# Moving the turns of probabilities and values inside the k and q units of a first attention

## The chip, the cores and the metric

One NeuronCore of a Trainium2 chip runs the whole program. The metric is the device time of one execution in microseconds. The four compute engines named here are TensorE (PE, with its weight loads shown as PEld), VectorE (DVE), ScalarE (ACT) and GpSimd (POOL); SyncE (SP) issues most of the DMAs. Every engine takes its instructions in the order in which the program wrote them for it, and they wait for one another through semaphores.

## The reference

Two transformer blocks in float32 for 512 tokens of width 1024. The change touches only the first block's differential attention, 8 heads, each with two softmaxes of 64 columns over causal scores; their difference multiplies 128 columns of values:

```python
qb = q.reshape(bsz, nb, Q_BLOCK, N_HEADS, 2, HEAD_DIM).transpose(1, 0, 2, 3, 4, 5)
def one_block(args):
    qblk, bi = args
    s = jnp.einsum('bqhcd,bkhcd->bhcqk', qblk, k).astype(jnp.float32) * scale
    s = jnp.where(mask, s, neg)
    p = jax.nn.softmax(s, axis=-1)
    a = p[:, :, 0] - lam * p[:, :, 1]
    return jnp.einsum('bhqk,bkhe->bqhe', a.astype(v.dtype), v)
# before it: q and k = rope(rmsnorm(q or k of the projection)), 64 columns at a time
# behind it: o = rmsnorm(o, subln_gain) * (1 - lam_init), then the output projection
```

## The kernel before

Work on TensorE comes in **units**: one unit is a 128-column slice of a projection, `named(name, ...)` or `tile` (L543), 8 slices k of the contraction with 3 matmuls of 512 columns each (L559 to L561; high and low halves of weights and activations), 24 matmuls into one of two PSUM banks `pg`. `ahead_of(k)` is called in front of each k. ScalarE splits a unit's weights into high and low halves three units ahead (`ahead`, `hi`, L1079 and L1080), GpSimd issues the accumulating DMA that makes the low half (L523), and SP loads raw weights and swaps halves of k and q for the rope (L495, L496).

The first attention is a loop over h from 1 to 9 with the units k, q and v of head h (gate units where no head is left) and, between them, the attention of head g = h - 1. Each engine has its own copy of the loop, and its order is written out by hand. The names of head g's steps:

- `scores(g, i)` (L733, L735): scores of query block i, two softmaxes, with the causal mask; it needs q after rope (`roped`) and a free bank `ps`. There are two banks `ps`; scores and turns take them in turn, so scores 0 and turn 2 of the head before share one, scores 2 and turn 0 share one, scores 1 and turn 3, scores 3 and turn 1.
- `maximum` (L1839) on VectorE, then `exps1` (L1221) on ScalarE, then `combine` (L1845, L1561, L1558; four instructions, result `pa`, semaphore `combed`) on VectorE.
- `turn(g, i)` (L743): i + 1 transposes of the combined block on TensorE into a bank `ps`; `turned` copies it to `pt`, turns 0 and 2 on ScalarE (L1233), turns 1 and 3 on VectorE (L1856).
- the values' turn (L801): four transposes of `v_raw` into `px`, copied by ScalarE (L1302).
- the product (L811): probabilities and values of head h - 2 into `py`; it waits for the copies of turns 2 and 3. ScalarE squares and copies `py` (L1311, L1312).
- `kq_out` (L1241, L1242): ScalarE's two evacuations of a k or q unit; `kq_rest` (two VectorE operations) makes the rest of its squares, `kq_sums` (L761, L762) sums them, `head_root` (L1252, L1254) takes the root; `rope_step` (four VectorE operations) applies it. The same for the output norm: `o_rest`, `o_sums` (L754, L755), L1248, and the product with the root on VectorE (L1558, `hid`).

The order before, per loop step h. TensorE: unit k; turns 2 and 3 of head h - 2; values' turn; scores 0 and 1; product of head h - 2; unit q; turns 0 and 1; sums of k; sums of the output norm; scores 2 and 3; unit v; sums of q. ScalarE: split; `kq_out` of k; copy of turn 2; copy of values; exponentials 0 and 1; copies of the product; split; `kq_out` of q; copy of turn 0; roots of k and of the output norm; exponentials 2 and 3; split; v; root of q. VectorE: copy of turn 3; rest of k; maxima 0 and 1; combines 0 and 1; rest of the output; copy of turn 1; rest of q; output norm; maxima 2 and 3; rope of k; combines 2 and 3; rope of q.

Of the kernel before, what the change touches and what calls it, by code (L numbers as in the profile page):

```python
# [7 lines left out]
P = 128  # L8
# [3 lines left out]
HEADS = 8  # L12
# [182 lines left out]
def build(nc, weights, x_dram, consts, rope, masks, params, ssm_b, ssm_c, lru_w, out):  # L195
    with ExitStack() as ctx:
# [209 lines left out]
        def evacuated(eng, name):  # L406

            eng.wait_ge(pg_free[TILE[name] % 2], TILE[name] // 2 + 1)
# [133 lines left out]
        def _(pe):  # L542
# [21 lines left out]
            def named(name, xh, xl, **kw):  # L564
                tile(UNIT[name], TILE[name], xh, xl, **kw)
# [33 lines left out]
            def x_use(name):  # L599
                if XUSE[name] > 0:  # L600
                    pe.wait_ge(px_free, XUSE[name])
# [126 lines left out]
            def scores(h, i):  # L728
                bank, w = s_use(("s", h, i)), P * (i + 1)
                pe.wait_ge(roped, 2 * h + 2)  # L730
                for c in range(2):
                    r = slice(64 * c, 64 * c + 64)
                    pe.matmul(bank[:, c, 0:w], qq[r, h % 2, P * i:P * i + P], kk[r, h % 2, 0:w], start=True, stop=False)  # L733
                for c in range(2):
                    last = pe.matmul(bank[:, c, P * i:w], ident_b, msk[:, M_TRI:M_TRI + P], start=False, stop=True)  # L735
                last.then_inc(ps_full, 1)

            def turn(h, i):

                bank = s_use(("t", h, i))  # L740
                pe.wait_ge(combed, 4 * h + i + 1)
                for j in range(i + 1):
                    last = pe.transpose(bank[:, 0, P * j:P * j + P], pa[:, i % 2, P * j:P * j + P], ident)  # L743
                last.then_inc(ps_full, 1)
# [37 lines left out]
                    pe.wait_ge(blocks_made, 1)  # L782
                    kq_sums(0, "k", 0)
            kq_sums(0, "q", 1)
            for h in range(1, HEADS + 2):
                g = h - 1
                attends = g < HEADS
                if h < HEADS:
                    named(("k", h), XH, XL)
                elif h == HEADS:  # L790
                    named(("gate", 4), XH, XL)
                else:
                    named(("gate", 7), XH, XL)
                if h >= 2:
                    turn(h - 2, 2)
                    turn(h - 2, 3)
                if attends:
                    x_use(("vt", g))
                    evacuated(pe, ("v", g))
                    for j in range(QB):  # L800
                        last = pe.transpose(px[:, P * j:P * j + P], v_raw[:, P * j:P * j + P], ident)  # L801
                    last.then_inc(px_full, 1)
                    scores(g, 0)
                    scores(g, 1)
                if h >= 2:
                    y_use(("pv", h - 2))
                    px_read(pe, ("vt", h - 2))
                    ps_read(pe, ("t", h - 2, 2))
                    ps_read(pe, ("t", h - 2, 3))
                    for j in range(QB):  # L810
                        last = pe.matmul(py[:, P * j:T], vv[:, h % 2, j, :], pt[:, j, P * j:T],  # L811
                                         start=j == 0, stop=j == QB - 1)
                    last.then_inc(py_full, 1)
                if h < HEADS:
                    named(("q", h), XH, XL)
                elif h == HEADS:
                    named(("gate", 5), XH, XL)
                if attends:
                    turn(g, 0)
                    turn(g, 1)  # L820
                if h < HEADS:
                    kq_sums(h, "k", 0)
                if 2 <= h <= HEADS:
                    o_sums(h - 2)
                if attends:
                    scores(g, 2)
                    scores(g, 3)
                if h < HEADS:
                    named(("v", h), XH, XL)
                    kq_sums(h, "q", 1)  # L830
                if h == HEADS:
                    named(("gate", 6), XH, XL)
# [229 lines left out]
        def _(act):  # L1062
# [198 lines left out]
                free(act.activation(hid[:, m], a, ACT.Sigmoid, bias=par("b_glu", m)), ("glu", m))  # L1261

            def late_gate(g):
                ahead(("gate", g))
                free(act.activation(gates[:, g], done(("gate", g)), ACT.Copy), ("gate", g))

            ahead(("k", 0))
# [22 lines left out]
            for h in range(1, HEADS + 2):  # L1290
                g = h - 1
                attends = g < HEADS
                if h < HEADS:
                    ahead(("k", h))
                    kq_out(h, "k", 0, "kg")
                else:
                    late_gate(4 if h == HEADS else 7)
                if h >= 2:
                    turned(h - 2, 2)
                if attends:  # L1300
                    px_ready(("vt", g))
                    act.activation(vv[:, g % 2], px[:].rearrange("p (j d) -> p j d", d=P), ACT.Copy).then_inc(px_free, 1)  # L1302
                    exps1(g, 0)
                    exps1(g, 1)
                if h == HEADS + 1:
                    act.wait_ge(maxed, EXPS[("s", HEADS - 1, QB - 1)] + 1)
                    for o in (5, 6):
                        o_high(o)
                if h >= 2:
                    py_ready(("pv", h - 2))  # L1310
                    put(act.activation(sq_hi[2] if h <= HEADS else nrm[:, 0], py[:], ACT.Square), o_sq)  # L1311
                    act.activation(hid[:, h - 2], py[:], ACT.Copy).then_inc(py_free, 1)  # L1312
                if h < HEADS:
                    ahead(("q", h))
                    kq_out(h, "q", 1, "qg")
                if h == HEADS:
                    late_gate(5)
                if attends:
                    turned(g, 0)
                if h == HEADS:  # L1320
                    for o in range(2):
                        o_high(o)
                if h < HEADS:
                    head_root(("ssq_k", h), 0, C_EPS, 1.0 / 64, rs_k)
                if h >= 2:
                    if h >= 3:
                        act.wait_ge(o_done, h - 2)
                    head_root(("ssq_o", h - 2), 2, C_EPS, 1.0 / P, rs_o)
                if attends:
                    exps1(g, 2)  # L1330
                    exps1(g, 3)
                if h < HEADS:
                    ahead(("v", h))
                    free(act.activation(v_raw[:], done(("v", h)), ACT.Copy), ("v", h))

                    head_root(("ssq_q", h), 1, C_EPS64, 1.0, rs_q)
                if h == HEADS:
                    for o in range(2, 5):
                        o_high(o)
                    late_gate(6)  # L1340

            o_high(HEADS - 1)
# [190 lines left out]
        def _(dve):  # L1533
# [366 lines left out]
            for h in range(1, HEADS + 2):  # L1900
                g = h - 1
                attends = g < HEADS
                if h >= 2:
                    turned(h - 2, 3)
                if h < HEADS:
                    kq_rest(h, "k", 0)
                if attends:
                    maximum(("s", g, 0), P, 0, soft)
                    maximum(("s", g, 1), 2 * P, 1, soft)
                    combine(g, 0)  # L1910
                    combine(g, 1)
                if 2 <= h <= HEADS:
                    o_rest(h - 2)
                if attends:
                    turned(g, 1)
                if h < HEADS:
                    kq_rest(h, "q", 1)
                if h == HEADS:
                    for o in range(2):
                        o_low(o)  # L1920
                if h == HEADS + 1:
                    for o in (5, 6):
                        o_low(o)
                if h >= 2:
                    py_read(dve, ("pv", h - 2))
                    dve.wait_ge(rs_o, h - 1)
                    put(stt(hid[:, h - 2], hid[:, h - 2], lam_t[:, 6:7], kq_rs[:, 2]), o_done)
                if attends:
                    maximum(("s", g, 2), 3 * P, 2, soft)
                    maximum(("s", g, 3), 4 * P, 3, soft)  # L1930
                if h < HEADS:
                    rope_step(h, "k", 0, rs_k, kk)
                if attends:
                    combine(g, 2)
                    combine(g, 3)
                if h < HEADS:
                    rope_step(h, "q", 1, rs_q, qq)
                if h == HEADS:
                    for o in range(2, 5):
                        o_low(o)  # L1940
# [361 lines left out]
```

## Time and profile before

| | |
|---|---|
| median of 3 runs | 1423.48 us (1423.08 to 1425.09) |
| the profiled execution | 1422.14 us, span 1420.3 us |
| TensorE busy | 1398.5 us, 98% of the span |
| ScalarE busy | 832.2 us, 59% |
| VectorE busy | 698.4 us, 49% |
| GpSimd busy | 202.0 us, 14% |
| granted TensorE clock | 0.999 |

A busy time is the sum of an engine's instructions over the span. Matmuls are pipelined: the duration of one (0.39 us) is longer than the distance to the next (0.23 us), so costs on TensorE are read from distances between starts, and idle time in brackets is what lies behind the modelled end of the instruction before.

### The profile page before, as it was taken

The numbers are of one execution on the slowest core, as the hardware profiler recorded it, in microseconds if no ns is written. First come the engines' busy times: TensorE is split into PE (matmuls) and PEld (weight loads), VectorE is DVE, ScalarE is ACT, GpSimd is POOL, SyncE is SP. The second block draws the span as 40 slices with busy tenths as digits, with TensorE's granted clock in tenths as the row PEclk, the third lists the DMA queues.
The fourth block names the chain that finished last, engine by engine and source line by source line (L and its number), as shares of the span: only waits on it lengthen the run. The fifth ranks groups of instructions, "written<-read, shape, count | busy, mean of one in ns | idle before, by whom it ended". The sixth has DMA issues, their size and how long they took to land.

```text
span 1420.3 us, 18417 instructions
## 1 busy us (share of the span) xinstructions
PE 1398.5 (98%) x6734; PEld 1121.1 (79%) x6734; DVE 698.4 (49%) x1228; ACT 832.2 (59%) x1174; POOL 202.0 (14%) x236
## 2 busy tenths in 40 slices
PE   7999999999999999999999999999999999999998
PEld 5887877777778888888888887777788888888887
DVE  6992477877734455544154165757465301213324
ACT  7536566776755656665365477645756655535442
POOL 1210100100111111111111111010101111111111
PEclk9999999999999999999999999999999999999999
DMA  9996966566579888888878997754667898888873
GB/s 298 221 188 154 233 156 141 132 156 142 115 197 220 193 188 193 187 202 192 214 177 187 214 233 158 160 139 108 145 153 162 193 202 192 190 202 180 206 163 89
DMA packets 82692, 254.76 MB, mean 179 GB/s; under 512 B 16816, under 2 KB 20016, under 8 KB 82608
## 3 DMA queue, kind: packets, MB, share of 16 engines
q0 software_dynamic: 32400, 117.98, 46.2%
q1 hardware_dynamic: 48768, 132.50, 30.9%
q10 hardware_dynamic: 1440, 3.15, 0.6%
q8 instruction: 54, 0.88, 0.3%
q14 instruction: 30, 0.25, 0.0%
HBM read 128.03 MB, written 3.41 MB: 93 GB/s over the span
## 4 chain that ended last, share of the span: by engine, by line
PE 94%; DVE 3%; ACT 2%; issue 0%; DMA 0%; DVEq 0%; ACTq 0%
PE pg L559 27%; PE pg L561 27%; PE pg L560 27%; PE ps L733 2%; PE py L811 1%; PE ps L947 1%; PE ps L957 1%; ACT pairs_r L1241 1%; PE py L967 1%; DVE acc L1558 1%; PE ps L735 0%; ACT kq_raw L1242 0%; PE ps L949 0%; DVE acc L1555 0%; PE px L632 0%
## 5 line engine op out<-in xcount | busy, mean ns | idle before, releaser
L559 PE MATMUL pg<-x_hi,w_hi 128*128 128x512 f32 x1088 | 429.0, 394 | 0.0
L561 PE MATMUL pg<-x_hi,w_lo 128*128 128x512 f32 x1088 | 424.0, 390 | 0.0
L560 PE MATMUL pg<-x_lo,w_hi 128*128 128x512 f32 x1088 | 423.5, 389 | 0.0
L523 POOL DMA_DIRECT2D w_lo<-w_raw x225 | 194.0, 862 | 1186.3 <-ACT w_lo L1080 1134.9
L1079 ACT ACTIVATE w_hi<-w_raw 128x1024 fp32r<-128x1024 f32 x222 | 233.4, 1051 | 100.9 <-PE pg L561 99.8
L559 PEld LDWEIGHTS pg<-x_hi,w_hi 128*128 128x128 f32 x1088 | 204.3, 188 | 43.5 <-issue 1.6
L561 PEld LDWEIGHTS pg<-x_hi,w_lo 128*128 128x128 f32 x1088 | 204.2, 188 | 43.0
L560 PEld LDWEIGHTS pg<-x_lo,w_hi 128*128 128x128 f32 x1088 | 204.4, 188 | 42.5 <-issue 1.0
L1080 ACT ACTIVATE w_lo<-w_raw 128x1024 fp32r<-128x1024 f32 x222 | 232.3, 1046 | 0.0
L559 PE MATMUL pg<-act_hi,w_hi 128*128 128x512 f32 x424 | 165.0, 389 | 0.0
L561 PE MATMUL pg<-act_hi,w_lo 128*128 128x512 f32 x424 | 165.0, 389 | 0.0
L560 PE MATMUL pg<-act_lo,w_hi 128*128 128x512 f32 x424 | 165.0, 389 | 0.0
L559 PEld LDWEIGHTS pg<-act_hi,w_hi 128*128 128x128 f32 x424 | 79.6, 188 | 16.8 <-DMA w_lo<-w_raw 0.2
L561 PEld LDWEIGHTS pg<-act_hi,w_lo 128*128 128x128 f32 x424 | 79.6, 188 | 16.6
L560 PEld LDWEIGHTS pg<-act_lo,w_hi 128*128 128x128 f32 x424 | 79.6, 188 | 16.3
L1555 DVE TENSOR_TENSOR cu<-pg,rstd 128x512 f32<-128x512 f32 x44 | 30.4, 691 | 114.6 <-PE pg L561 112.9
L1555 DVE TENSOR_TENSOR pairs<-rel 128x512 f32<-128x512 f32 x30 | 20.8, 692 | 129.5 <-ACT rel L1500 129.5
L1555 DVE TENSOR_TENSOR hid<-hid,pg 128x512 f32<-128x512 f32 x32 | 22.0, 687 | 102.8 <-PE pg L561 98.8
L1558 DVE SCALAR_TENSOR_TENSOR cnv<-cu,prm,cnv 128x511 f32<-128x511 f32 x88 | 66.0, 750 | 3.1
L1555 DVE TENSOR_TENSOR acc<-acc,pg 128x512 f32<-128x512 f32 (+1 forms) x24 | 16.2, 676 | 92.1 <-PE pg L561 91.3
L1221 ACT ACTIVATE pr<-ps,soft 128x128 f32<-128x128 f32 (+3 forms) x64 | 33.2, 523 | 27.1 <-DVE soft L1839 26.4
L1839 DVE TENSOR_REDUCE soft<-ps 128x2 f32<-128x256 f32 (+3 forms) x48 | 39.6, 824 | 6.7 <-PE ps L949 4.1
(384 smaller groups left out, 1743.9 us busy)
## 6 DMA issues: line engine op xcount, KB each, us to landing
w_raw<-weights SPq DMA_DIRECT2D x226, 512.0 KB, 4.8
w_lo<-w_raw POOLq DMA_DIRECT2D x225, 512.0 KB, 5.7
kq_rot<-kq_raw SPq DMA_DIRECT2D x64, 64.0 KB, 3.3
hid<-x SPq DMA_DIRECT2D x4, 512.0 KB, 5.4
hid<-x ACTq DMA_DIRECT2D x8, 256.0 KB, 5.3
out<-hid SPq DMA_DIRECT2D x16, 128.0 KB, 1.8
u_dram<-hid SPq DMA_DIRECT2D x4, 256.0 KB, 5.4
pairs<-u_dram SPq DMA_DIRECT2D x8, 128.0 KB, 6.8
```

The source lines that it names most:

```text
L523: pool.dma_start(w_lo[:, s], w_raw[:, s], accum_op=ALU.add).then_inc(lo_in[s], 16)
L559: pe.matmul(bank[:], wh, xh(k), start=n == 0, stop=False)
L560: pe.matmul(bank[:], wh, xl(k), start=False, stop=False)
L561: last = pe.matmul(bank[:], wl, xh(k), start=False, stop=n == len(ks) - 1)
L733: pe.matmul(bank[:, c, 0:w], qq[r, h % 2, P * i:P * i + P], kk[r, h % 2, 0:w], start=True, stop=False)
L811: last = pe.matmul(py[:, P * j:T], vv[:, h % 2, j, :], pt[:, j, P * j:T], start=j == 0, stop=j == QB - 1)
L1079: act.activation(w_hi[:, s], w_raw[:, s], ACT.Copy)
L1080: put(act.activation(w_lo[:, s], w_raw[:, s], ACT.Copy, scale=-1.0), hi_done)
L1221: ins = act.activation(dst[:, c, 0:w], bank[:, c, 0:w], ACT.Exp, bias=negmax[:, i % 2, c:c + 1], **kw)
L1555: return dve.tensor_tensor(out_, a, b, op)
L1558: return dve.scalar_tensor_tensor(out_, a, s, b, op0, op1)
L1839: put(dve.tensor_reduce(s[:, i % 2, 0:2], bank[:, :, 0:w], AX.X, ALU.max, negate=True), maxed)
```

## The change

Three orders are changed, one per engine; no instruction of arithmetic is added or dropped. TensorE: turns 2 and 3 of head h - 2 and the values' turn are called in front of k = 6 of unit k, turns 0 and 1 of head g in front of k = 7 of unit q, and the product comes ahead of scores 0 and 1. ScalarE: the copies of turn 2 and of the values come ahead of k's evacuations, the copy of turn 0 ahead of q's. VectorE: maxima 0 and 1 come ahead of the rest of k's squares. `late_gate` no longer calls `ahead`; its callers do.

```diff
+            def values_of(h):
                 if h >= 2:
                     y_use(("pv", h - 2))
...
+            for h in range(1, HEADS + 2):
+                g = h - 1
+                attends = g < HEADS
+
+                def last_turns(k):
+                    if k != 6:
+                        return
+                    if h >= 2:
+                        turn(h - 2, 2)
+                        turn(h - 2, 3)
+                    if attends:
+                        x_use(("vt", g))
+                        evacuated(pe, ("v", g))
+                        for j in range(QB):
+                            last = pe.transpose(px[:, P * j:P * j + P], v_raw[:, P * j:P * j + P], ident)
+                        last.then_inc(px_full, 1)
+
+                def first_turns(k):
+                    if k == 7 and attends:
+                        turn(g, 0)
+                        turn(g, 1)
+
+                named(("k", h) if h < HEADS else ("gate", 4 if h == HEADS else 7), XH, XL, ahead_of=last_turns)
+                values_of(h)
                 if attends:
-                    turn(g, 0)
-                    turn(g, 1)
+                    scores(g, 0)
+                    scores(g, 1)
+                if h <= HEADS:
+                    named(("q", h) if h < HEADS else ("gate", 5), XH, XL, ahead_of=first_turns)
                 if h < HEADS:
                     kq_sums(h, "k", 0)
...
             for h in range(1, HEADS + 2):
                 g = h - 1
                 attends = g < HEADS
-                if h < HEADS:
-                    ahead(("k", h))
-                    kq_out(h, "k", 0, "kg")
-                else:
-                    late_gate(4 if h == HEADS else 7)
+                ahead(("k", h) if h < HEADS else ("gate", 4 if h == HEADS else 7))
                 if h >= 2:
                     turned(h - 2, 2)
                 if attends:
                     px_ready(("vt", g))
                     act.activation(vv[:, g % 2], px[:].rearrange("p (j d) -> p j d", d=P), ACT.Copy).then_inc(px_free, 1)
+                if h < HEADS:
+                    kq_out(h, "k", 0, "kg")
+                else:
+                    late_gate(4 if h == HEADS else 7)
+                if attends:
                     exps1(g, 0)
                     exps1(g, 1)
...
+                if h <= HEADS:
+                    ahead(("q", h) if h < HEADS else ("gate", 5))
+                if attends:
+                    turned(g, 0)
                 if h < HEADS:
-                    ahead(("q", h))
                     kq_out(h, "q", 1, "qg")
                 if h == HEADS:
                     late_gate(5)
-                if attends:
-                    turned(g, 0)
-                if h == HEADS:
                     for o in range(2):
                         o_high(o)
...
                 if h >= 2:
                     turned(h - 2, 3)
+                if attends:
+                    maximum(("s", g, 0), P, 0, soft)
+                    maximum(("s", g, 1), 2 * P, 1, soft)
                 if h < HEADS:
                     kq_rest(h, "k", 0)
                 if attends:
-                    maximum(("s", g, 0), P, 0, soft)
-                    maximum(("s", g, 1), 2 * P, 1, soft)
                     combine(g, 0)
                     combine(g, 1)
```

## Rows read from the trace of the kernel before

**Rows 1.** The page: its span, and the chain that ended last by engine

```profile
span 1420.3 us, 18417 instructions
...
PE 94%; DVE 3%; ACT 2%; issue 0%; DMA 0%; DVEq 0%; ACTq 0%
```

**Rows 2.** Stretches: busy us and count per engine, clock, DMA share, GB/s; head 4

```profile
258.00:284.00 26.00, 25.55 (x126) 18.97 (x125) 20.17 (x37) 18.52 (x38) 2.57 (x4) 1.00 0.62 142
```

**Rows 3.** Timeline, TensorE, head 4: start, duration, engine, line, operation, idle before

```profile
258.41 0.93 PE L743 MATMUL ps<-cst,pa 128*128 128x128 f32 x7
...
259.17 0.60 PE L801 MATMUL px<-cst,v_raw 128*128 128x128 f32 x4
...
260.13 0.49 PE L733 MATMUL ps<-kk,qq 64*128 64x128 f32 x4 [0.36 <-ACT pt L1233]
...
263.66 0.48 PE L559 MATMUL pg<-x_hi,w_hi 128*128 128x512 f32 x1
...
263.97 0.40 PE L560 MATMUL pg<-x_lo,w_hi 128*128 128x512 f32 x1
...
269.24 0.49 PE L743 MATMUL ps<-cst,pa 128*128 128x128 f32 x3
...
269.49 0.47 PE L761 MATMUL px<-pairs_r,blocks 128*128 128x512 f32 x1
...
270.75 0.92 PE L733 MATMUL ps<-kk,qq 64*128 64x384 f32 x4
...
272.96 0.48 PE L559 MATMUL pg<-x_hi,w_hi 128*128 128x512 f32 x1
...
284.42 0.92 PE L743 MATMUL ps<-cst,pa 128*128 128x128 f32 x7
```

**Rows 4.** Timeline, TensorE, head 8: values' turn and scores 0

```profile
363.20 0.60 PE L801 MATMUL px<-cst,v_raw 128*128 128x128 f32 x4
363.73 0.49 PE L733 MATMUL ps<-kk,qq 64*128 64x128 f32 x4
```

**Rows 5.** Timeline, TensorE, head 1: scores 2

```profile
192.71 0.92 PE L733 MATMUL ps<-kk,qq 64*128 64x384 f32 x4 [0.55 <-ACT pt L1233]
```

**Rows 6.** Timeline, VectorE, from the output norm in head 4 to head 5

```profile
273.30 0.75 DVE L1558 SCALAR_TENSOR_TENSOR hid<-hid,lam_t,kq_rs 128x512 f32<-128x512 f32 x1 [1.25 <-ACT kq_rs L1254]
274.08 2.22 DVE L1839 TENSOR_REDUCE soft<-ps 128x2 f32<-128x768 f32 x2
...
281.77 0.75 DVE L1558 SCALAR_TENSOR_TENSOR pa<-pr,soft 128x512 f32<-128x512 f32 x1
282.56 0.75 DVE L1558 SCALAR_TENSOR_TENSOR rope_a<-kq_raw,prm,rtab 128x512 f32<-128x512 f32 x1
...
285.45 0.69 DVE L1856 COPY pt<-ps 128x512 f32<-128x512 f32 x1
286.18 0.69 DVE L1555 TENSOR_TENSOR pairs<-kq_raw 128x512 f32<-128x512 f32 x1
```

**Rows 7.** Timeline, ScalarE, head 4, behind the q unit

```profile
269.44 0.60 ACT L1241 ACTIVATE pairs_r<-pg 128x512 fp32r<-128x512 f32 x1 [2.52 <-PE pg L561]
...
270.41 0.28 ACT L1233 ACTIVATE pt<-ps 128x128 f32<-128x128 f32 x1
...
272.54 0.63 ACT L1254 ACTIVATE kq_rs<-kq_rs 128x512 f32<-128x512 f32 x1
```

**Rows 8.** Timeline, VectorE and TensorE, head 9: last copy and product

```profile
388.11 0.69 DVE L1856 COPY pt<-ps 128x512 f32<-128x512 f32 x1 [3.29 <-PE ps L743]
...
388.95 2.39 PE L811 MATMUL py<-pt,vv 128*128 128x512 f32 x8 [0.94 <-DVE pt L1856]
```

**Rows 9.** Timeline, VectorE, head 8: maximum 1 and the end of combine 1

```profile
365.39 0.69 DVE L1839 TENSOR_REDUCE soft<-ps 128x2 f32<-128x512 f32 x1 [0.43 <-PE ps L735]
...
368.13 0.48 DVE L1558 SCALAR_TENSOR_TENSOR pa<-pr,soft 128x256 f32<-128x256 f32 x1
```

**Rows 10.** Timeline, VectorE, head 1: the last operation of q's rope

```profile
204.88 0.69 DVE L1555 TENSOR_TENSOR qq<-rope_a,kq_rs 128x512 f32<-128x512 f32 x1
```

More of the change, by code:

```diff
@@ L784, in _ @@
             kq_sums(0, "q", 1)
-            for h in range(1, HEADS + 2):
-                g = h - 1
-                attends = g < HEADS
-                if h < HEADS:
-                    named(("k", h), XH, XL)
-                elif h == HEADS:
-                    named(("gate", 4), XH, XL)
-                else:
[L793 to L796, printed above, removed]
-                if attends:
[L798 to L804, printed above, removed]
+            def values_of(h):
                 if h >= 2:
@@ L813, in _ @@
                     last.then_inc(py_full, 1)
[L814 to L817, printed above, removed]
+            for h in range(1, HEADS + 2):
[19 more added lines that the diff above has]
+                values_of(h)
                 if attends:
-                    turn(g, 0)
-                    turn(g, 1)
+                    scores(g, 0)
+                    scores(g, 1)
+                if h <= HEADS:
+                    named(("q", h) if h < HEADS else ("gate", 5), XH, XL, ahead_of=first_turns)
                 if h < HEADS:
@@ L1263, in late_gate @@
             def late_gate(g):
-                ahead(("gate", g))
                 free(act.activation(gates[:, g], done(("gate", g)), ACT.Copy), ("gate", g))
@@ L1292, in _ @@
                 attends = g < HEADS
-                if h < HEADS:
-                    ahead(("k", h))
-                    kq_out(h, "k", 0, "kg")
-                else:
-                    late_gate(4 if h == HEADS else 7)
+                ahead(("k", h) if h < HEADS else ("gate", 4 if h == HEADS else 7))
                 if h >= 2:
@@ L1317, in _ @@
                     late_gate(5)
-                if attends:
-                    turned(g, 0)
-                if h == HEADS:
                     for o in range(2):
@@ L1339, in _ @@
                         o_high(o)
+                    ahead(("gate", 6))
                     late_gate(6)
```

## The prediction

> **What bounds the kernel now.** I read the page's chain that ended last first: 94% of it lies on TensorE, in a span of 1420.3 us [rows 1]. Only what shortens TensorE's stream can shorten the kernel. The change touches one stretch, the first attention (178 to 391 us), so the second view is the table of stretches: one head takes 26.00 us, TensorE is busy in 25.55 of it at full granted clock (1.00), VectorE in 20.17, ScalarE in 18.52 [rows 2]. Six stretches of 26.00 between 206 and 362 look like it. TensorE has almost no idle time there, so the whole prize is a few tenths per head, and a chain through VectorE that is busy 78% of the time can take it back.
>
> The third view is TensorE's timeline in one head [rows 3]. Behind the k unit stand seven turns of probabilities (258.41 to 259.17, 0.76), four turns of values, the scores 0 and 1, and the product of probabilities and values. The scores begin at 260.13, 0.96 after the values' turns. In head 8 the same step is 0.53 [rows 4]. The difference, **0.43 us, is a wait** for ScalarE's copy L1233, which comes behind the two evacuations of k on ScalarE. Behind the q unit the turns take 0.25 (269.24 to 269.49), and from there to the scores 2 it is 1.26 us, where four sum matmuls stand. The first of them costs 0.31, as 263.66 to 263.97 shows for a matmul behind such a block, and the others some 0.235: 1.01. The rest is **a wait of 0.24** for the same line. In head 1, with two sums, it is 0.71: the row shows 0.55 of idle behind the modelled end of the last sum, and a modelled end lies 0.16 behind the end of issue (0.39 against 0.23) [rows 5].
>
> **What each part of the change does on TensorE.** No instruction of arithmetic is added or removed; all of them move. I count starts, so a block's cost is the distance between its first row and the next block's.
>
> - The turns of probabilities and values go in front of k = 6 of the k unit, with 6 matmuls behind them. They cost what they do now, but without the pause between value turns and scores: 0.76 + 0.36 = 1.12 instead of 0.76 + 0.53. Going back to unit matmuls costs once more what it costs at 263.66, where the second matmul comes 0.31 after the first instead of 0.227: 0.08, and some hundredths behind it, 0.11 in all. TensorE therefore pays 1.23 instead of 1.72 (with the wait of 0.43). Bounds of the restart: 0 (no restart), and 0.13, by which a fresh unit (263.66 to 269.24, 5.58) is longer than a k unit of 24 x 0.227 = 5.45.
> - The turns 0 and 1 go in front of k = 7 of the q unit: 0.25 + 0.10 of restart. In exchange the sums behind the unit run at 0.235 each (0.94) instead of 1.01 + 0.24 of wait, since ScalarE copies the turned block before it evacuates q.
> - The product of probabilities and values is put ahead of the scores: same length, 260.13 to 263.66 = 3.53 for both together.
>
> If nothing else waited, a head would be 1.23 + 3.53 + 5.58 + 0.35 + 0.94 + 2.21 (scores 2 and 3, 270.75 to 272.96) + 11.46 (v unit, q sums, k unit, 272.96 to 284.42) = **25.30 against 26.01 now** (258.41 to 284.42): 0.71 less.
>
> **What is late next.** The product needs the block turned last, and its copy is VectorE's (L1856). Today it has time: the scores stand between. In the changed order only six matmuls do. On VectorE this copy comes behind the whole rope step of q, and the rows from 273.30 to 285.45 stand without a gap: output norm, maxima 2 and 3, rope of k, combine 2 and 3 (done at 282.52), rope of q, copy until 286.14 [rows 6]. That is 12.84 us, and the change moves nothing in it. It starts when ScalarE has finished the root for the output norm. Take Q as the end of issue of the q unit (269.24). ScalarE starts on it 0.20 later and ends the last root (272.54 + 0.63) at Q + 3.93 [rows 7]; without the 128-column copy between them, some 0.15 (270.41 to 270.56, where the next operation begins), at Q + 3.78; VectorE starts 0.13 behind: Q + 3.91. The copy is then done at Q + 16.75. From a copy's end to the product it was 0.15 in head 9 (388.80 to 388.95) [rows 8], so the product can start at **Q + 16.90**. TensorE gets there at Q + 0.94 + 2.21 + 11.46 + 1.23 = **Q + 15.84**. So it waits 1.06 us, and a head takes 25.30 + 1.06 = **26.36, 0.35 more than now**. The two waits removed (0.67) come back as one larger wait, because the loop (root, norm, maxima, two ropes, copy, product, scores, q unit) is closed: what TensorE saves elsewhere in the head only makes it arrive earlier at this wait. Queued behind the waiting product are the scores 0 and 1 and so the next maxima; VectorE's idle time moves there, since the rest of k's squares is now behind the maxima.
>
> A second place is close. Turn 1, in front of k = 7, needs combine 1. Counted from the start of scores 0: maximum 1 is done 2.39 later (363.73 to 366.12, which is 365.39 + 0.69 and a gap of 0.04) [rows 4, 9]; then the rest of k's squares, two operations of 0.69 with gaps, 1.42 [rows 6]; then two combines, 366.12 to 368.61 [rows 9]: 6.30, and 0.15 of latency. TensorE asks at 1.39 + 4.90 (21 matmuls, 5.58 less three at 0.227) + 0.11 = 6.40. That is a wait of 0.05 per head. Its bounds are 0 and 0.3.
>
> The other queues: ScalarE's weight split for the unit three ahead moves at most 1.7 us later in the q unit, and it is needed some 26 us later; POOL and SP follow it with the same reserve. k's evacuation waits for TensorE's unit end and is not behind anything by then. I cost these at nothing; the cover is those 26 us.
>
> **The sum by heads**, against the profiled execution.
> Head 1: 0.71 of wait gone, 0.07 and 0.08 at the two joints saved, 0.10 of restart paid, -0.76. Head 2: VectorE's chain starts without the output norm and its wait, rope of q ends at 205.57, some 14.1 us behind the q unit of head 1 [rows 10]; with the copy and the latency that is 15.0, and TensorE asks at 15.4: -0.71. Heads 3 to 7: +0.35 to +0.40 each, +1.9. Head 8 has no wait of 0.43 today (its k unit is a gate unit with one evacuation) but gets the 1.06: +1.06 - 0.06 there, -0.13 behind the q unit, +0.87. Head 9: today the product waits 1.1 for the same copy (0.94 of it idle in the row, 0.16 up to the end of issue) [rows 8], and VectorE, idle for 3.29 before, can only begin it when the turn is there; in the changed kernel the turns come 1.47 ahead of the product (six matmuls and the restart), and begin to end of the copy with its latencies is 1.1: -1.07 with the restart. Total: -0.76 - 0.71 + 1.9 + 0.87 - 1.07 = **+0.2 us**; with the bounds above (restarts of 0 in eight heads, 0.3 for turn 1 in eight heads), -1.5 to +2.5. I take +0.5, as small restarts and latencies have been counted low more easily than high. The profiled execution took 1422.14 us (1420.3 of span), and the median of the runs is 1423.48, 1.34 more; the forecast is made for the median: 1423.48 + 0.5 = **1424.0 us**. About 0.2%, 2.85 us, is what a measurement of this kernel can tell from no change.
>
> **Rivals.**
> *The waits simply go.* If VectorE's copy is not behind the rope of q in time, or the chain starts earlier than Q + 3.91, the product finds its block ready. Then head 1 gives 0.76, heads 2 to 7 give 0.71 each, head 8 gives 0.19, head 9 1.07: 6.3 less, 1417.2 us; with half of the wait left, 1420. For it: TensorE holds 94% of the chain and its idle rows name only ScalarE's copy. Against it: the rows without a gap on VectorE. The Trainium skill (Perfetto Trace Analysis, "Identifying the Most-Contended Engine") says to optimize the engine with the highest occupancy first, and its next section to follow the gaps on it; by that rule the gaps named here are the gain, and the 78% on VectorE would not decide. The rows of the chain speak against that here. Chance 0.13.
>
> *Slower through the first combine.* The rest of k's squares now stands between maximum 1 and combine 0, and turn 1 in front of k = 7 has a reserve of nothing. From the first tenth by which the exponentials or the combine come later than counted, TensorE stands still inside the q unit, one for one. If it is 0.4 per head, as much as one wait for L1233 costs today, eight heads pay 3.2: 1427.2 us. Its place is the first turn with line L743 inside the q unit, its releaser VectorE. For it: nothing is left in reserve. Against it: in the changed order ScalarE has nothing else between the maxima and the exponentials, and VectorE gives it the 1.42 us of k's squares as a lead. Chance 0.14.
>
> **How the numbers follow.** Forecast case 0.73, its own range 1422.3 to 1426.3; full or half gain 0.13; slower 0.14. The range 1420.3 to 1426.9 leaves out about one in ten on each side. Faster by over 0.2% 0.13, within 0.73, slower 0.14.
>
> **What would show it.** Right: heads 3 to 8 with a period near 26.4, no idle time in front of the scores, and about 1 us in front of the product (L811's code) with VectorE's copy as releaser, right behind the rope's last operation; head 9 without a wait. Wrong: a period of 25.3 (the chain on VectorE does not hold), or idle time in front of the turns inside the q unit (the second rival), or a changed time in stretches behind 391 us, for which I have no cause.

## The result and the profile after

| | before | changed |
|---|---|---|
| median | 1423.26 us (20 runs, 1422.42 to 1425.09) | 1425.69 us (20 runs, 1424.6 to 1426.84) |
| ratio to before, 95% interval | | 1.0016 [1.0009, 1.0022] |
| span of the profiled execution | 1420.3 us | 1422.4 us |
| start of the output projection behind the attention | 391.10 us | 393.13 us |
| one head, heads 3 to 7 | 26.00 us | 26.63 us |
| from the output projection's start to the end of the span | 1029.2 us | 1029.3 us |

The changed kernel is 2.4 us, 0.16%, slower. That is inside the 0.2% that the prediction called no change, but the interval lies wholly above 1: the slowdown is small and real. In the traces 2.0 of the 2.1 us lie in the first attention; behind it they run alike.

The page of the changed kernel, its span and its chain by engine:

```profile
span 1422.4 us, 18413 instructions
...
PE 87%; DVE 9%; ACT 2%; issue 1%; DMA 0%; SPq 0%; DVEq 0%; ACTq 0%
```

TensorE's share of the chain fell from 94% [rows 1] to 87% and VectorE's rose from 3% to 9%: a chain through VectorE has become part of what ends last. The table of waits for TensorE between 175 and 400 us (engine, line, whom it waited for: total, times, longest) names it:

```profile
PE py L793 <- DVE pt L1862: 4.1, 6, 0.7
PE pg L559 <- DVE pairs_r L1561: 0.4, 1, 0.4
```

Six waits of the product (L793 here, L811 before) for VectorE's copy of the block turned last (L1862, before L1856), one in each of the heads 3 to 8. The wait for ScalarE's copy in front of the scores is gone. In TensorE's timeline, from head 4 to head 5, against [rows 3]:

```profile
256.93 0.93 PE L743 MATMUL ps<-cst,pa 128*128 128x128 f32 x7
...
270.11 0.39 PE L761 MATMUL px<-pairs_r,blocks 128*128 128x512 f32 x1
...
270.62 0.47 PE L754 MATMUL py<-pairs_r,blocks 128*128 128x512 f32 x1
270.93 0.40 PE L755 MATMUL py<-sq_lo,blocks 128*128 128x512 f32 x1
271.25 0.92 PE L733 MATMUL ps<-kk,qq 64*128 64x384 f32 x4
...
283.56 0.93 PE L743 MATMUL ps<-cst,pa 128*128 128x128 f32 x7
...
284.68 0.48 PE L559 MATMUL pg<-x_hi,w_hi 128*128 128x512 f32 x1
...
287.00 2.39 PE L793 MATMUL py<-pt,vv 128*128 128x512 f32 x8 [0.68 <-DVE pt L1862]
289.33 0.49 PE L733 MATMUL ps<-kk,qq 64*128 64x128 f32 x4
...
290.70 0.47 PE L559 MATMUL pg<-x_hi,w_hi 128*128 128x512 f32 x1
...
295.57 0.63 PE L743 MATMUL ps<-cst,pa 128*128 128x128 f32 x3
295.96 0.48 PE L559 MATMUL pg<-x_hi,w_hi 128*128 128x512 f32 x1
```

Seven turns come at 256.93 and again at 283.56: 26.63. The six matmuls behind the values' turns (from 284.68, 1.47 us) would be through at 286.15; the product starts at 287.00, a wait of 0.85 (0.68 behind the modelled end). VectorE in the same stretch, against [rows 6]:

```profile
269.78 0.69 DVE L1561 TENSOR_TENSOR sq_lo<-pairs,pairs_r 128x512 fp32r<-128x512 f32 x1
...
274.00 0.75 DVE L1564 SCALAR_TENSOR_TENSOR hid<-hid,lam_t,kq_rs 128x512 f32<-128x512 f32 x1 [1.09 <-ACT kq_rs L1259]
274.79 2.22 DVE L1845 TENSOR_REDUCE soft<-ps 128x2 f32<-128x768 f32 x2
...
283.26 0.75 DVE L1564 SCALAR_TENSOR_TENSOR rope_a<-kq_raw,prm,rtab 128x512 f32<-128x512 f32 x1
...
286.16 0.69 DVE L1862 COPY pt<-ps 128x512 f32<-128x512 f32 x1
290.14 0.42 DVE L1845 TENSOR_REDUCE soft<-ps 128x2 f32<-128x256 f32 x1 [3.29 <-PE ps L735]
```

The copy ends at 286.85 and the product follows 0.15 later. With Q, the end of issue of the q unit, at 270.11, where the sums begin, the norm starts at Q + 3.89, the copy is done at Q + 16.74 and the product starts at Q + 16.89. VectorE then stands idle for 3.29 us, because the scores are queued behind the waiting product.

Where the 2.0 us between the traces come from, by the starts of the k units:

| | before | changed | difference | predicted |
|---|---|---|---|---|
| head 1 | 22.67 | 22.23 | -0.44 | -0.76 |
| head 2 | 26.01 | 25.72 | -0.29 | -0.71 |
| heads 3 to 7 | 130.03 | 133.13 | +3.10 | +1.9 |
| head 8 | 24.63 | 25.45 | +0.82 | +0.87 |
| head 9, to the output projection | 9.48 | 8.30 | -1.18 | -1.07 |

### The profile page after: what moved, and what is told of

Its sections match the earlier page's. It is cut to its first block, busy times and chain, and to the rows that moved or that the text cites. A ratio compares the mean times of both kernels' runs of the same rounds, so it can differ in the third digit from the quotient of the medians.

```text
span 1422.4 us, 18413 instructions
## 1 busy us (share of the span) xinstructions
PE 1399.6 (98%) x6730; PEld 1119.5 (79%) x6734; DVE 698.2 (49%) x1228; ACT 834.3 (59%) x1174; POOL 202.0 (14%) x236
## 4 chain that ended last, share of the span: by engine, by line
PE 87%; DVE 9%; ACT 2%; issue 1%; DMA 0%; SPq 0%; DVEq 0%; ACTq 0%
PE pg L559 26%; PE pg L561 26%; PE pg L560 26%; PE py L793 1%; DVE soft L1845 1%; PE ps L733 1%; PE ps L952 1%; PE ps L962 1%; DVE rope_a L1564 1%; DVE rope_a L1561 1%; DVE pa L1564 1%; DVE kq_rot L1564 1%; PE py L972 1%; DVE acc L1564 1%; DMA hid<-x 0%
```

## The experiments

**Theory A**: in heads 3 to 8 the loop is closed by VectorE's chain (output norm, maxima, two ropes, copy of turn 3); the product, now directly behind the k unit, waits for it. **Theory B**, the rival: VectorE has idle time enough, and the moved blocks simply cost TensorE more where they stand now. Where an expectation speaks of a second place, it means turn 1 inside the q unit, which may wait for combine 1. Medians of the kernel before, on the chips of these runs, were 1423.1 to 1423.6 us.

### The chain made shorter: the output norm behind the maxima

```diff
-                if h >= 2:
-                    py_read(dve, ("pv", h - 2))
-                    dve.wait_ge(rs_o, h - 1)
-                    put(stt(hid[:, h - 2], hid[:, h - 2], lam_t[:, 6:7], kq_rs[:, 2]), o_done)
                 if attends:
                     maximum(("s", g, 2), 3 * P, 2, soft)
                     maximum(("s", g, 3), 4 * P, 3, soft)
+                if h >= 2:
+                    py_read(dve, ("pv", h - 2))
+                    dve.wait_ge(rs_o, h - 1)
+                    put(stt(hid[:, h - 2], hid[:, h - 2], lam_t[:, 6:7], kq_rs[:, 2]), o_done)
```

> The changed kernel with VectorE's output norm moved behind maxima 2 and 3. Theory A (VectorE's chain from the norm to the copy of turn 3 sets the loop): VectorE no longer waits 1.09 us for ScalarE's root before the maxima, the copy ends about 1.06 us earlier, and the wait of about 0.85 in front of the product is gone in heads 3 to 8. 6 x 0.85 = 5.1 us less than the changed kernel: 1420.6 us, ratio to the kernel before 0.998. Theory B (the turns inside the units and the product ahead of the scores simply cost TensorE more, whatever VectorE does): no change, 1425.7 us.

1419.77 us against 1423.4, ratio 0.9974 [0.9965, 0.9983]; a head takes 25.72. VectorE and TensorE in this kernel, head 4 to 5:

```profile
272.03 2.22 DVE L1845 TENSOR_REDUCE soft<-ps 128x2 f32<-128x768 f32 x2
274.28 0.75 DVE L1564 SCALAR_TENSOR_TENSOR hid<-hid,lam_t,kq_rs 128x512 f32<-128x512 f32 x1
...
284.19 0.69 DVE L1862 COPY pt<-ps 128x512 f32<-128x512 f32 x1
```

```profile
285.25 2.32 PE L793 MATMUL py<-pt,vv 128*128 128x512 f32 x8
```

The maxima no longer stand behind the root of the output norm (no idle time in brackets). The sums begin at 269.19 here, so the copy, done at 284.88, is done at Q + 15.69, 1.05 earlier than in the changed kernel, and the product starts at 285.25 without a wait. TensorE's program is that of the changed kernel to the instruction, so theory B falls: 0.91 us per head, 5.9 us between the medians, came from the order of three VectorE instructions.

### The cover put back: the product behind the scores

```diff
                 named(("k", h) if h < HEADS else ("gate", 4 if h == HEADS else 7), XH, XL, ahead_of=last_turns)
-                values_of(h)
                 if attends:
                     scores(g, 0)
                     scores(g, 1)
+                values_of(h)
```

> The changed kernel with the product back behind scores 0 and 1; all else stays. Theory A: the scores cover the copy as they did before. They wait only some 0.1 for the rope of q, and the q unit starts 0.9 us earlier than in the changed kernel; turn 1 also gets a reserve. About 1.0 less in each of heads 3 to 8 and 0.2 in the others: 1419 to 1420 us. Theory B: only the 0.17 per head by which the pair product, scores is longer than scores, product comes back, 1.3 us: 1424.4 us.

1419.52 us, ratio 0.9971 [0.9959, 0.9983]; a head takes 25.62, 1.01 less than in the changed kernel. TensorE, then VectorE:

```profile
281.31 0.93 PE L743 MATMUL ps<-cst,pa 128*128 128x128 f32 x7
...
284.15 0.49 PE L733 MATMUL ps<-kk,qq 64*128 64x128 f32 x4
...
285.55 2.38 PE L793 MATMUL py<-pt,vv 128*128 128x512 f32 x8
```

```profile
283.31 0.69 DVE L1561 TENSOR_TENSOR qq<-rope_a,kq_rs 128x512 f32<-128x512 f32 x1
284.04 0.69 DVE L1862 COPY pt<-ps 128x512 f32<-128x512 f32 x1
```

The scores need only the rope, which ends at 284.00, and follow 0.15 later; the copy ends at 284.73 behind them, 0.8 before the product wants it. With this one move undone, the kernel is 3.9 us faster than before instead of 2.4 us slower. It is what makes the change a loss; the smaller costs of the other moves are read further below.

### The copy ahead of the rope of q

```diff
                 if attends:
                     combine(g, 2)
                     combine(g, 3)
+                    turned(g, 3)
                 if h < HEADS:
                     rope_step(h, "q", 1, rs_q, qq)
```

(and it is gone from the head of the loop)

> The changed kernel with VectorE's copy of turn 3 ahead of the rope of q instead of behind it. Theory A: the copy ends about 1.5 us earlier, the product finds its block ready; the rope ends later (about 18.1 us behind the q unit's end), just before TensorE reaches the scores (18.4). 0.85 less in heads 3 to 8: 1420.6 us. If the rope comes later than counted, a wait in front of the scores takes the product's place one for one. Theory B: 1425.7 us.

1420.43 us, ratio 0.9976 [0.9966, 0.9987]; a head takes 25.71, as with the shorter chain. VectorE now waits 1.37 us for the turn, and the rope still comes in time:

```profile
283.36 0.69 DVE L1862 COPY pt<-ps 128x512 f32<-128x512 f32 x1 [1.37 <-PE ps L743]
284.09 0.75 DVE L1564 SCALAR_TENSOR_TENSOR rope_a<-kq_raw,prm,rtab 128x512 f32<-128x512 f32 x1
```

So it is the place of this one copy behind the rope that held the product. Three ways of taking the wait away give the same head to 0.11 us.

### The chain made longer, in the changed kernel and in the one before

```diff
                 if h < HEADS:
+                    tt_(sq_full, mult, mult)
                     rope_step(h, "q", 1, rs_q, qq)
```

In the changed kernel:

> The changed kernel with one more VectorE operation of 512 columns (about 0.73 us) per head in front of the rope of q; its result is used by nothing. Theory A: the chain is the loop, so heads 3 to 8 get longer by the whole 0.73, head 2 by some 0.3: 4.7 us, 1430.4 us. Theory B: VectorE has 6 us of idle time per head, no change: 1425.7 us.

1428.95 us against 1423.14, ratio 1.004 [1.0025, 1.0056]. VectorE, then TensorE:

```profile
284.86 0.69 DVE L1561 TENSOR_TENSOR pairs<-cst 128x512 f32<-128x512 f32 x1
285.47 0.74 DVE L1564 SCALAR_TENSOR_TENSOR rope_a<-kq_raw,prm,rtab 128x512 f32<-128x512 f32 x1
```

```profile
289.20 2.40 PE L793 MATMUL py<-pt,vv 128*128 128x512 f32 x8 [1.27 <-DVE pt L1862]
```

The operation takes 0.61 from its start to the next one's, not the 0.73 of the expectation; the head grows from 26.63 to 27.23, by 0.60, one for one within the reading. The whole first attention grows by 3.85 in the traces, and the medians by 3.3, where 4.7 were expected; the shorter operation accounts for some 0.7 of that. In the kernel before:

> The kernel before with the same additional VectorE operation in front of the rope of q. Theory A: the scores cover the copy here; only the rope itself passes the scores' present start by 0.1 to 0.2. 0.15 in each of heads 2 to 7, about 1 us: 1424.2 us. If VectorE were the loop's bound in the kernel before as well: 0.73 x 6 = 4.4 us, 1427.7 us.

1423.6 us against 1423.14, ratio 1.0005 [0.9995, 1.0014], a head 26.03. The waits of TensorE in this kernel, 175 to 400 us:

```profile
PE ps L733 <- ACT pt L1233: 2.9, 7, 0.5
PE py L811 <- DVE pt L1856: 0.9, 1, 0.9
PE pg L559 <- DVE pairs_r L1555: 0.4, 1, 0.4
PE ps L733 <- DVE qq L1555: 0.4, 1, 0.4
```

The same 0.6 us on the same engine costs 0.60 per head in one kernel and 0.03 in the other. That is the difference between a loop without and with cover. The cover is not large, though. The rope and the scores of head 4 to 5, first in the kernel before, then in this run:

```profile
284.73 0.69 DVE L1555 TENSOR_TENSOR qq<-rope_a,kq_rs 128x512 f32<-128x512 f32 x1
```

```profile
286.14 0.49 PE L733 MATMUL ps<-kk,qq 64*128 64x128 f32 x4 [0.36 <-ACT pt L1233]
```

```profile
285.76 0.69 DVE L1555 TENSOR_TENSOR qq<-rope_a,kq_rs 128x512 f32<-128x512 f32 x1
```

```profile
286.60 0.49 PE L733 MATMUL ps<-kk,qq 64*128 64x128 f32 x4 [0.39 <-ACT pt L1233]
```

Before, the rope ended at 285.42; with 0.15 to the scores it had 0.57 to spare behind the wait for ScalarE's copy. The added 0.61 uses that up: the rope ends at 286.45, and the scores start 0.15 later, although the profile still names ScalarE. A longer operation would have cost time in this kernel too. In head 8, where the scores had no such wait, it does: the row with qq is there, and heads 8 and 9 together take 0.47 more. The expected 0.15 per head was an overestimate.

### The shorter chain in the kernel before

The edit is that of the first experiment.

> The kernel before with VectorE's output norm moved behind maxima 2 and 3, nothing else. Theory A: in the kernel before the scores wait for ScalarE's copy, and VectorE's chain has cover, so a shorter chain gives nothing: 26.0 us per head, 1423.3 us. Rival (moving the norm is good by itself, wherever the bound is): 3 to 4 us less, as it gave in the changed kernel: about 1420 us.

1423.3 us against 1423.6, ratio 0.9999 [0.999, 1.0008], a head 26.01. The edit that gave 5.9 us behind the change gives nothing ahead of it: the chain on VectorE was not the bound there; with the change it is.

### The rest of k's squares ahead of the maxima

```diff
-                if attends:
-                    maximum(("s", g, 0), P, 0, soft)
-                    maximum(("s", g, 1), 2 * P, 1, soft)
                 if h < HEADS:
                     kq_rest(h, "k", 0)
                 if attends:
+                    maximum(("s", g, 0), P, 0, soft)
+                    maximum(("s", g, 1), 2 * P, 1, soft)
                     combine(g, 0)
```

> The changed kernel with the rest of k's squares back ahead of maxima 0 and 1 on VectorE. Theory A, second place: in the changed kernel turn 1 inside the q unit waits about 0.1 for combine 1, because 1.42 us of squares stand between; in front of the maxima they fall into 3.3 us of idle time of VectorE. The three turns take 0.25 instead of 0.39, 0.1 to 0.14 less per head, 0.8 to 1.0 in all: 1424.8 us. Rival (the 0.39 is what transposes cost inside a unit): 1425.7 us, three turns still 0.39.

1424.88 us, ratio to before 1.0009 [1.0, 1.0018]; a head takes 26.49, 0.14 less than in the changed kernel. TensorE, turns inside the q unit up to the sums:

```profile
269.09 0.49 PE L743 MATMUL ps<-cst,pa 128*128 128x128 f32 x3
...
270.11 0.39 PE L761 MATMUL px<-pairs_r,blocks 128*128 128x512 f32 x1
...
271.12 0.92 PE L733 MATMUL ps<-kk,qq 64*128 64x384 f32 x4
```

From the turns to the sums it is 1.02 instead of 1.18 (295.57 to 296.75) in the changed kernel. In the changed kernel turn 1 did wait for combine 1, some 0.15 and not 0.05 per head. The four sums and the step to the scores also shrink, from 1.14 to 1.01: in the changed kernel the third sum, the first of the output norm, starts at 270.62, 0.15 behind the end of VectorE's second squares operation (270.47). The product's wait stays (0.81 in brackets), and head 1 gets 0.26 longer, where k's squares come late and turn 1 waits 0.21 for VectorE; heads 8 and 9 together get 0.15 longer.

### ScalarE's order alone

The kernel before, with ScalarE's copies of turns 2 and 0 ahead of the evacuations; TensorE and VectorE as before. The copy of the values keeps its old place, behind k's evacuations.

```diff
+                ahead(("k", h) if h < HEADS else ("gate", 4 if h == HEADS else 7))
+                if h >= 2:
+                    turned(h - 2, 2)
                 if h < HEADS:
-                    ahead(("k", h))
                     kq_out(h, "k", 0, "kg")
                 else:
                     late_gate(4 if h == HEADS else 7)
-                if h >= 2:
-                    turned(h - 2, 2)
...
+                if h <= HEADS:
+                    ahead(("q", h) if h < HEADS else ("gate", 5))
+                if attends:
+                    turned(g, 0)
                 if h < HEADS:
-                    ahead(("q", h))
                     kq_out(h, "q", 1, "qg")
                 if h == HEADS:
                     late_gate(5)
-                if attends:
-                    turned(g, 0)
...
```

> The kernel before with the new order of ScalarE alone: the copies of turns 2 and 0 ahead of the evacuations of k and q; TensorE and VectorE keep the order of before, all turns stay behind the units. Theory A: the wait of 0.43 in front of scores 0 and of about 0.15 in front of scores 2 goes; ScalarE evacuates q about 0.3 later, and the rope of q comes to bind the scores by 0.2 to 0.3. 25.6 to 25.7 us per head, 2 to 3 us less in all: 1420.8 us. Rival (ScalarE's copy cannot come earlier without the turns inside the units, since it then waits for TensorE): no change, 1423.3 us.

1419.39 us against 1423.6, ratio 0.997 [0.996, 0.9981]; a head takes 25.55. TensorE, then ScalarE and VectorE:

```profile
282.24 0.93 PE L743 MATMUL ps<-cst,pa 128*128 128x128 f32 x7
283.00 0.60 PE L801 MATMUL px<-cst,v_raw 128*128 128x128 f32 x4
283.66 0.49 PE L733 MATMUL ps<-kk,qq 64*128 64x128 f32 x4
```

```profile
282.76 0.49 ACT L1233 ACTIVATE pt<-ps 128x384 f32<-128x384 f32 x1 [1.33 <-PE ps L743]
283.15 0.59 ACT L1241 ACTIVATE pairs_r<-pg 128x512 fp32r<-128x512 f32 x1
```

```profile
282.82 0.69 DVE L1556 TENSOR_TENSOR qq<-rope_a,kq_rs 128x512 f32<-128x512 f32 x1
```

The values' turns to the scores take 0.66 instead of 0.96 [rows 3]; 0.53 would be no wait [rows 4], and the 0.13 left is the rope of q, which ends at 283.51, 0.15 before the scores (the last row, VectorE). One engine's order brings more than was expected of it (1420.8), and as much as the whole change does with the product put back (1419.52). The product ahead of the scores takes it back.

### Two combinations

The changed kernel with the output norm later and the product behind the scores:

> The changed kernel with both edits, the output norm behind maxima 2 and 3 and the product back behind scores 0 and 1. Theory A: no engine is waited for any more in heads 3 to 8; a head is about 25.5 us against 26.0 before and 26.6 in the changed kernel, so 1418 to 1419 us. Theory B: 1424.4 us.

1418.22 us against 1423.14, ratio 0.9962 [0.9949, 0.9976]; a head takes 25.48, no wait in heads 3 to 8. And on the kernel before, ScalarE's order with the output norm later:

> As the run with ScalarE's order alone, and VectorE's output norm behind maxima 2 and 3. Theory A: the chain of VectorE ends 1 us earlier and the scores wait for nothing; without the restarts inside the units a head is about 25.4 us: 1418 to 1419 us, as good as the best of the other runs. If the turns inside the units are needed for the gain: 1420.8 us.

1419.18 us against 1423.6, ratio 0.9968 [0.9956, 0.998]; a head takes 25.43. Per head this is the shortest, so the turns inside the k and q units give nothing in a head of the loop's middle; they even cost the 0.05 between 25.43 and 25.48. What this kernel keeps is the wait in head 9:

```profile
383.15 0.92 PE L743 MATMUL ps<-cst,pa 128*128 128x128 f32 x7
385.02 2.39 PE L811 MATMUL py<-pt,vv 128*128 128x512 f32 x8 [0.95 <-DVE pt L1857]
```

There, and only there, nothing stands between turns and product. The last kernel puts the turns inside the unit in head 9 alone:

```diff
+                def last_turns(k):
+                    if k == 6:
+                        turn(h - 2, 2)
+                        turn(h - 2, 3)
...
-                    named(("gate", 7), XH, XL)
-                if h >= 2:
+                    named(("gate", 7), XH, XL, ahead_of=last_turns)
+                if 2 <= h <= HEADS:
                     turn(h - 2, 2)
                     turn(h - 2, 3)
```

> ScalarE's order and the later output norm on the kernel before, and the turns 2 and 3 in front of k = 6 only in head 9, where the product waited 1.1 us for VectorE's copy. Theory A: there nothing else stands between turn and product, so six matmuls are the right cover: 1.0 less than the run without it, about 25.4 us per head, 1418.0 us. Rival (the chain behind the last product takes it back): no change, 1419.2 us.

**1417.8 us against 1423.61, ratio 0.9959 [0.9945, 0.9972]**, the lowest median of this study, 5.8 us below the one before and 7.9 below the changed one. From the turns to the end of the product's issue:

```profile
382.13 0.93 PE L743 MATMUL ps<-cst,pa 128*128 128x128 f32 x7
...
384.28 2.32 PE L816 MATMUL py<-pt,vv 128*128 128x512 f32 x8
```

Turns to product 2.15 with six matmuls (1.47) between them, where it was 1.87 without any; the wait is gone. From head 1's k unit to the output projection it takes 207.4 us, against 208.6 in the run before it. Whether it beats the first combination (1418.22) can't be said: the intervals overlap.

## Why the prediction was right, and where its sum was off

**The forecast** of a change below 0.2% held, by the mechanism it named. The time of 1424.0 us was 1.7 short, and the slowdown was 2.4 us where 0.5 was forecast. Between the traces it was 2.0 where the sum gave 0.2. That is still inside the sum's bounds of -1.5 to +2.5, and in part by luck: the room upwards was meant for turn 1 alone, and over half of what was missing came from terms that had been given no bounds.

**The waits that go, and the one that comes.** Predicted: no idle time in front of the scores, and the product waiting for VectorE's copy behind the rope of q, released at Q + 16.90. Measured: Q + 16.89, by the same steps (norm at Q + 3.89 against 3.91, copy done at Q + 16.74 against 16.75). The experiments show it as cause: shorten the chain by 1.05 and the wait is gone, lengthen it by 0.61 and the head grows by 0.60, and neither moves the kernel before by more than 0.03 in a head of the loop's middle.

**The size of the wait** was 0.85 and not 1.06. TensorE reached the product at Q + 16.04 instead of Q + 15.84, for the four sums and the step to the scores took 1.14 instead of 0.94: some 0.13 at the third sum, late for VectorE's squares, and the rest at the step to the scores. Inside this loop that costs nothing; the wait takes it up.

**The head's length** came out 26.63 instead of 26.36 to 26.41, and this is the mis-sized term. Two pieces stand behind the wait and count in full. Product and scores together were set at 3.53, the same as scores and product, with no bounds; they take 3.70 (287.00 to 290.70). And the part from the q unit's start to the sums was 5.93, it takes 6.05: turn 1's wait for combine 1 was put at 0.05 and is about 0.15. Over heads 3 to 7 that is 1.2 us of the 1.8 that were missing between the traces (2.0 measured, 0.2 summed).

**Heads 1 and 2** gave 0.44 and 0.29 where 0.76 and 0.71 were summed. The prize had been read too large: behind float32r sums the step to the scores takes 0.32 with no wait at all (270.93 to 271.25 in the changed kernel), so of the 0.24 put down as a wait in front of scores 2 only some 0.15 was one. In head 1 the restart and the wait for combine 1 inside the q unit took 0.22 where 0.10 had been paid, and the values' turn inside the k unit cost 0.04 where 0.07 were to be saved. In head 2, where the product does not wait, as forecast, the late third sum (0.13), the product ahead of the scores (0.09) and turn 1 (0.11) are the rest.

**Head 8 and head 9** came out about as summed, +0.82 and -1.18. Head 9 is the one place where a turn inside a unit is worth its restart, and the last experiment shows it alone.

**The rivals.** That the waits simply go, and the gain with them, is what the kernel does as soon as the product stands behind the scores or the norm behind the maxima: 1419.5 and 1419.8 against the 1417.2 worked out for it. The Trainium skill (Perfetto Trace Analysis, "Identifying the Most-Contended Engine") says to optimize the engine with the highest occupancy first. The runs agree with it on the prize: TensorE's waits for L1233, taken away by ScalarE's order alone, were worth 4.2 us. What it did not tell is that in the changed order a chain on VectorE, busy 78% of a head, would hold the product. The second rival, slower through the first combine, was real and small: about 0.14 per head, as the run with the squares ahead of the maxima shows; at 0.4 it had been put too high.

**What would show it.** A period near 26.4 (26.63), about 1 us in front of the product (0.85), head 9 without a wait, nothing changed behind the attention: all as named, the first with the size that was off.

What stays open: why product and scores take 0.17 more in the new order. In the run with the later norm, where the product does not wait, product to scores takes 2.25, and the scores up to the unit 1.37, together 3.62; so 0.09 come with the order. The other 0.08 are seen only where the product has waited (2.33 from product to scores). Both were read from starts, and no run takes them apart further.

## What to carry to other kernels

Before moving a consumer up to close a gap, write down for each of its inputs when it is done, counted along the in-order queue of the engine that makes it; what stood between producer and consumer was cover for the slowest of them, here a copy behind a rope step on an engine that was idle a fifth of the time. When a wait is one engine's order (a copy behind two evacuations), mend that order first and measure it alone: the order of one engine out of three was worth 4.2 us, and the rest of the change cost 6.3. Test a suspected loop by adding one operation to it, before and after: 0.60 per head against 0.03 settles it in two runs. Read the slack beside it, for the answer holds only for the length that was added: here 0.61 against 0.57.

## What the runs showed of the hardware

A VectorE operation of 512 float32 columns whose result nobody waits for took 0.61 us from its start to the next one's, with a duration of 0.69 in the trace. Where the kernel waits for the result, as between the last operation of the rope and the copy, the same step was 0.72 to 0.73. And on TensorE the step from one matmul to the next, 0.23 between float32r matmuls of 512 columns, was longer where the kind changed: 0.32 from the last sum to the first score, and 0.31 from the first to the second matmul of a unit that follows scores, turns or products.
